# Retention outputs leave PSUM normalised by ScalarE instead of VectorE

## The reference, cut to what matters

```python
def retention(q, k, v, gn_g):
    ...
    scores = jnp.einsum('bnihd,bnjhd->bnhij', qc, kc) * decay
    inner = jnp.einsum('bnhij,bnjhe->bnihe', scores, vc)
    ...
    cross = jnp.einsum('bnihd,ih,bnhde->bnihe', qc, q_w, R_prev)
    o = (inner + cross).reshape(B, L, H, DV)
    mu = jnp.mean(o, axis=-1, keepdims=True)
    var = jnp.mean(jnp.square(o - mu), axis=-1, keepdims=True)
    o = ((o - mu) * lax.rsqrt(var + EPS)).reshape(B, L, H * DV)
    return o * gn_g.astype(jnp.float32)
...
    ret = retention(q, k, v, ret_gn_g[l]).astype(x.dtype) * jax.nn.silu(g_ret)
```

## Time and profile before

| | us |
|---|---|
| median of three runs | 2453.55 |
| the three runs | 2453.55, 2457.36, 2446.6 |
| the profiled execution, its own time | 2457.15 |
| its span, from the first to the last instruction | 2455.3 |
| busy in it: TensorE, VectorE, ScalarE, GpSimd | 2377.6, 1449.8, 679.2, 192.3 |
| mean granted TensorE clock | 0.992 of full speed |

### The profile page before, as it was taken

How to read it: one execution, slowest core, us unless ns; L and a number is a source line. 1 busy time by engine, 2 the same in 40 slices (tenths; PEclk the granted TensorE clock), 3 DMA queues, 4 the chain that set the end, 5 groups by cost and what they waited for, 6 DMA issues and landing times.

```text
span 2455.3 us, 35223 instructions
## 1 busy us (share of the span) xinstructions
PE 2377.6 (97%) x14746; PEld 1980.7 (81%) x14746; DVE 1449.8 (59%) x2462; ACT 679.2 (28%) x1096; POOL 192.3 (8%) x89
## 2 busy tenths in 40 slices
PE   7999999999999999999999998889999999999998
PEld 5887888887888788988877886777888888888887
DVE  5785259928896241471623542665566657777777
ACT  4211122124221021151423426341244432121123
POOL 1100000000000240202000000001000000000000
PEclk9999999999999999999999999999999999999999
DMA  7345652255577516332053342122145556434442
GB/s 232 124 143 178 211 173 102 90 188 177 172 243 222 178 56 214 137 108 103 22 206 100 122 164 84 55 76 104 51 169 187 181 200 215 139 136 137 133 146 90
DMA packets 269202, 354.30 MB, mean 144 GB/s; under 512 B 34962, under 2 KB 159859, under 8 KB 269043
## 3 DMA queue, kind: packets, MB, share of 16 engines
q1 hardware_dynamic: 236066, 301.56, 37.0%
q10 hardware_dynamic: 32976, 50.48, 5.6%
HBM read 244.93 MB, written 107.05 MB: 143 GB/s over the span
## 4 chain that ended last, share of the span: by engine, by line
PE 77%; DVE 10%; DMA 5%; ACT 3%; issue 3%; SPq 1%; ACTq 0%; DVEq 0%
PE PS L518 23%; PE PS L521 18%; PE PS L3381 14%; PE PS L3461 9%; DMA LAR<-ret_d 1%; PE PS L697 1%; DMA RAW<-in_w_gate_up 1%; PE PS L1966 1%; DVE W_LO L416 1%; PE PS L1982 1%; PE PS L2591 1%; DMA x_d<-X 1%; PE PS L1319 1%; PE PS L2586 1%; DMA CB<-pch_d 1%
## 5 line engine op out<-in xcount | busy, mean ns | idle before, releaser
L518 PE MATMUL PS<-W_HI,OP_HI 128*128 128x512 f32 (+1 forms) x1152 | 294.9, 399 | 3.2 <-DVE XO L1507 3.2
L518 PE MATMUL PS<-W_LO,OP_HI 128*128 128x512 f32 (+1 forms) x1152 | 280.1, 385 | 1.0 <-DVE W_LO L416 1.0
L518 PE MATMUL PS<-W_HI,OP_LO 128*128 128x512 f32 (+1 forms) x1152 | 278.9, 384 | 0.0
L451 POOL TENSOR_SCALAR W_HI<-RAW 128x2048 fp32r<-128x2048 f32 (+1 forms) x66 | 131.7, 2009 | 1528.6 <-PE PS L518 672.6
L518 PEld LDWEIGHTS PS<-W_LO,OP_HI 128*128 128x128 f32 x1152 | 213.9, 189 | 45.0 <-DVE W_LO L416 1.4
L518 PEld LDWEIGHTS PS<-W_HI,OP_HI 128*128 128x128 f32 x1152 | 209.9, 191 | 47.0 <-DVE OP_LO L1468 3.6
L518 PEld LDWEIGHTS PS<-W_HI,OP_LO 128*128 128x128 f32 x1152 | 212.6, 188 | 42.8 <-issue 0.5
L547 ACT ACTIVATE OST<-PS 128x512 f32<-128x512 f32 (+2 forms) x152 | 85.8, 564 | 440.8 <-PE PS L521 241.8
L416 DVE TENSOR_TENSOR W_LO<-RAW,W_HI 128x2048 fp32r<-128x2048 f32 (+1 forms) x58 | 138.5, 2405 | 81.1 <-POOL W_HI L451 61.7
L521 PE MATMUL PS<-OP_HI,W_HI 128*128 128x512 f32 x704 | 180.5, 398 | 0.0
L521 PE MATMUL PS<-OP_HI,W_LO 128*128 128x512 f32 x704 | 174.4, 390 | 0.0
(11 more groups left out here) (529 smaller groups left out, 3728.3 us busy)
## 6 DMA issues: line engine op xcount, KB each, us to landing
RAW<-in_w_gate_up SPq DMA_DIRECT2D x88, 512.0 KB, 5.9
RAW<-in_w_in SPq DMA_DIRECT2D x28, 1024.0 KB, 6.6
RAW<-in_w_out SPq DMA_DIRECT2D x12, 1024.0 KB, 8.5
LE<-spill_d SPq DMA_DIRECT2D x22, 512.0 KB, 4.5
RAWD<-in_w_down SPq DMA_DIRECT2D x11, 1024.0 KB, 4.9
X<-x_d SPq DMA_DIRECT2D x4, 2048.0 KB, 8.8
x_d<-X SPq DMA_DIRECT2D x2, 4096.0 KB, 18.2
ptok_d<-OST ACTq DMA_DIRECT2D x24, 256.0 KB, 2.0
```

The costliest lines, as they stand in the source:

```text
L451: nc.gpsimd.tensor_scalar(hi, raw, 1.0, 1.0, ALU.mult, ALU.mult).then_inc(*w_hi.by(1))
L518: ins = nc.tensor.matmul(PS[:, bank, 0:width], act_part[:, k, a * P:(a + 1) * P], w_part[:, slot, k, 0:width], start=start, stop=stop)
```

## The change: who writes the normalised outputs

The variance, its root and the reciprocal stay where they were. VectorE then forms, for all heads at once, minus the mean times the reciprocal root (`RNB`, 128 by 8), and signals `r_on`. ScalarE waits for that and writes `ONR`, head by head, with the function Identity, with the reciprocal root as the scale and `RNB` as the bias, each of them one number per partition; then it signals `r_on` again, which therefore counts to 2 per tile. The second signal is the one that TensorE waits for.

```diff
--- before.py
+++ after.py
@@ -68,7 +68,7 @@
 
 for later, earlier, total in (e.split() for e in (
         "gm r_turn 8, dec r_sc 8, tr r_o 8, la r_kv 7, c1 xw_lo 8, ex r_qkt 8, rt r_root 8, trc xv_hi 8, e1 r_trig 2,"
-        "ag r_scr 8, ss r_var 8, kk r_on 8, s r_rst 8, lt r_g 8, ct r_ang 1, in0 rq_in 128, in1 rv_in 128, v0 glu_z 16,"
+        "ag r_scr 8, ss r_var 8, kk r_on 16, s r_rst 8, lt r_g 8, ct r_ang 1, in0 rq_in 128, in1 rv_in 128, v0 glu_z 16,"
         "par rc_in 32,av s5_prm_t 1,q s5_cp_t 1").split(",")):
     SHARED["dn_" + later] = (earlier, int(total))
 
@@ -1605,6 +1605,7 @@
     BNS = at("BNS", "small", 2560, [P, RH, 6])
     BNM = at("BNM", "small", 2752, [P, RH, 2])
     RRS = at("RRS", "small", 2816, [P, 3, RH])
+    RNB = at("RNB", "small", 2912, [P, RH])
 
     rc_in, rq_in, rv_in, rg_in, rt_out = (sem(n) for n in ("rc_in", "rq_in", "rv_in", "rg_in", "rt_out"))
     r_ang, r_trig, r_ab, r_rot, r_turn, r_qkt, r_sc, r_scr, r_o, r_kv = (
@@ -1686,7 +1687,7 @@
             pe.wait_ge(*rv_in(16 * (t + 1)))
             pe.wait_ge(*r_rst(t + 1))
             if t:
-                pe.wait_ge(*r_on(t))
+                pe.wait_ge(*r_on(2 * t))
             place = lambda h: PS[:, 4 + h % 2, h // 2 * P:(h // 2 + 1) * P]
             for h in range(RH):
                 T.matmul(place(h), SCR[:, h % 2, h // 2, :], VL[:, h * P:(h + 1) * P], start=h < 2, stop=False)
@@ -1703,7 +1704,7 @@
             ins.then_inc(*r_kv.by(1))
 
         def turn_out(t):
-            pe.wait_ge(*r_on(t + 1))
+            pe.wait_ge(*r_on(2 * t + 2))
             if t + 1 < TT:
                 pe.wait_ge(*r_scr(t + 2))
             else:
@@ -1747,6 +1748,14 @@
             yield ret_time(t) + 0.6
             act.wait_ge(*r_var(t + 1))
             act.activation(RRS[:, 1, :], RRS[:, 0, :], ACT.Sqrt).then_inc(*r_root.by(1))
+            yield ret_time(t) + 0.8
+            act.wait_ge(*r_on(2 * t + 1))
+            if t:
+                act.wait_ge(*r_back(t))
+            for h in range(RH):
+                ins = act.activation(ONR[:, h, :], PS[:, 4 + h % 2, (h // 2) * P:(h // 2 + 1) * P], ACT.Identity,
+                                     bias=RNB[:, h:h + 1], scale=RRS[:, 2, h:h + 1])
+            ins.then_inc(*r_on.by(1))
             if t + 1 < TT:
                 yield ret_time(t) + 1.2
                 turned(t + 1)
@@ -1814,13 +1823,10 @@
 
         def normalize(t):
             dve.wait_ge(*r_root(t + 1))
+            if t:
+                dve.wait_ge(*r_on(2 * t))
             chain(V.reciprocal(RRS[:, 2, :], RRS[:, 1, :]))
-            if t:
-                dve.wait_ge(*r_back(t))
-            for h in range(RH):
-                ins = V.tensor_scalar(ONR[:, h, :], PS[:, 4 + h % 2, (h // 2) * P:(h // 2 + 1) * P],
-                                      BNM[:, h, 0:1], RRS[:, 2, h:h + 1], SUB, MUL)
-            ins.then_inc(*r_on.by(1))
+            V.scalar_tensor_tensor(RNB[:, :], BNM[:, :, 0], -1.0, RRS[:, 2, :], MUL, MUL).then_inc(*r_on.by(1))
 
         def gate(t):
             dve.wait_ge(*r_back(t + 1))
```

## The result

The changed kernel takes 2468.68 us (median of six runs, 2463.11 to 2473.7) where the kernel before, run beside it, takes 2454.32 (six runs, 2446.6 to 2457.36): 1.0058 times as long, with an interval of 1.0046 to 1.0071. In a later comparison it was 2471.14 against 2452.55, a ratio of 1.0080 [1.0065, 1.0095]. It is slower, by 14.4 and 18.6 us; forecast were 16.2. The profiled execution of the change took 2470.99, its span is 2469.2 and its mean clock 0.991.

A forecast was written before the change was run, and what follows sets the result against it. ScalarE's list order was taken to bound: the eight delay the sigmoid and `QKT`, so TensorE waits. Tile costs 4.6 + 2.6 + 2.0 + 4.8 + 0.3 + 1.9 = 16.2 on 2453.55 give about 2470 us, range 2457 to 2479.

The forecast's parts named there:

- ScalarE's list is what bounds: Main case, chance 0.66: ScalarE's list order is fixed and every tile lacks room, so slower, about 2470 us.
- the share of 28%: ScalarE's busy share, set aside as its room; 1.35 us in hand before tile 0's scores was taken instead.
- The price of the row: ScalarE's eight normalising instructions per tile: 455 ns each (278 + 89 + 88), 3.01 us a row; `RNB` on VectorE 0.20.
- the two cheaper rows: Lower prices for ScalarE's eight, 1.57 and 2.29 us a row, giving sums of 7.1 and 12.3 us.
- The waits: TensorE before the next scores, held by ScalarE's `QKT`: 3.03, 5.03, 2.0, 4.5, 0.3, 1.9 us at tiles 0-4 and 6.
- Mask waits go, VectorE idles before `GA`: TensorE's mask waits of 2.47 and 1.34 us vanish; VectorE's 2.4 us saved per tile goes into waiting for `GA`.
- The falls of the clock: TensorE's clock drops after longer waits, 1.6 us each, counted at tiles 0, 1 and 3.
- its upper end: Upper sum of 21.6 us: 16.2 plus 3.2 for falls at tiles 2 and 6 and 2.2 for tile 4.
- The end, with its 3.18, I take to move along: TensorE's 3.18 us wait before 818.46 stays, since loads and weight splits there wait on TensorE's units.
- the third case: Rival, chance 0.08: the end wait shrinks if loads do not move with TensorE, 16.2 - 3.2 - 1.7 = 11.3, so 2465 us.

The follow-up runs named there:

- a row of 1.47: The changed kernel with ScalarE's eight instructions copying without scale and bias, so outputs are not normalised: 2454.65 us, 1.0009 of the kernel before.
- the first profile: Profiled execution of the changed kernel (normalisation moved to ScalarE, against the kernel before): 2470.99 us; median of its six runs 2468.68.
- the second: The changed kernel run again unaltered, for a second profile: profiled execution 2474.18 us, median of six runs 2471.14, against 2452.55 before.

## Why the prediction was right, and where its steps were not

- **ScalarE's list is what bounds.** Right, and shown by place alone: 2442.5 with the eight behind, 2468.7 to 2471.1 with them in front. The view to read was the list, and not the share of 28%.
- **The price of the row.** 455 forecast, 465 measured; row 2.90 for 3.01; `RNB` 0.17 for 0.20. (By its own terms the two cheaper rows were 1.59 and 2.31, not 1.57 and 2.29, which changes nothing.) The rule of the Trainium skill (ScalarE: Activation LUTs, "What ACT_TABLE_LOAD costs") gave an estimate of 479 with two operands, and for none 293: the trace has 465 and 303. The rule of the Trainium skill that speaks for moving an eviction (VectorE: DVE Perf Modes, "Specifications") agrees only without operands, 303 against VectorE's 405, which has its two; with two, ScalarE's 465 is the dearer one. The time per instruction did not decide whether the kernel became slower: the same row stands in the slowest and in the fastest kernel here. Where the row stands in front of the others, it sets how much: 2454.65 with a row of 1.47.
- **The waits.** 3.0, 5.0, 2.0, 4.5, 0.3, 1.9 forecast; 1.82, 4.86, 1.77, 3.86, 1.35, 1.94 in the first profile and 2.93, 4.86, 1.78, 3.86, 0.54, 1.95 in the second. Tile 0's 1.82 is the first execution's own: TensorE came 1.3 late to it from the longer fall at 599.65. Of tile 3's 4.5, 0.6 were too many. Tile 4 was named as the uncertain one, with bounds of 0 and 2.5.
- **Mask waits go, VectorE idles before `GA`.** Right: behind the first mask none in either profile, and 19.7 us of idle time, in before 4.1 by the same view. The experiment with the copy in front showed what the prediction hadn't: once `QKT` no longer hid them, `GA` alone cost mask waits of 5.12 and 7.31, 3.3 of the latter beside GpSimd.
- **The falls of the clock.** Forecast behind tiles 0, 1 and 3. The first profile has them behind 1 and 3, the second behind five waits. Behind waits of about 1.8 to 2.0 it came or didn't; the prediction kept that for its upper end.
- **"The end, with its 3.18, I take to move along": this step failed.** The end gave 6.0 back in both profiles of the change, which is the third case, with a chance of 0.08. Its price of 3.2 + 1.7 was right for the wait and 1.1 too low for the fall. Both profiled executions came out near the 2470 all the same (2470.99 and 2474.18), since something stood against it each time: in the second extra falls at tiles 2 and 6 and a growth of 20.4 instead of 16.2, besides 2.3 ahead of the stretch and 2.8 behind it, which were not followed; in the first the 6.0 of entry and first fall. So the number was hit partly by luck, by errors of opposite sign; the direction was not.

**How the end went.** In the kernel before, VectorE's timeline has

```profile
813.29 4.42 DVE L1468 TENSOR_TENSOR OP_LO<-LAR,OP_HI 128x1024 fp32r<-128x1024 f32 x1 [7.58 <-ACT OP_HI L1462]
817.64 0.68 DVE L1507 TENSOR_TENSOR XO<-XI,PS 128x512 f32<-128x512 f32 x1
```

and GpSimd's, in the same kernel,

```profile
812.05 4.58 POOL L457 TENSOR_TENSOR W_LO<-RAW,W_HI 128x2048 fp32r<-128x2048 f32 x1
```

The split that takes 1.23 alone ended 1.1 after GpSimd's product did, at 817.71, and `XO`, for which TensorE waited, stood behind it. GpSimd's timeline of the changed kernel:

```profile
831.95 5.59 POOL L457 TENSOR_TENSOR W_LO<-RAW,W_HI 128x2048 fp32r<-128x2048 f32 x1
```

Here VectorE's split began at 831.85, 0.10 ahead; it took 1.23, and GpSimd's product became 1.0 longer. Against the last `turn_out`, GpSimd began at the same time in both kernels (14.15 behind it) and VectorE's split 1.3 earlier. In all seven profiles with `ONR` on ScalarE the split was first, by 0.06 to 0.98, and took 1.23 to 1.90; in both of the kernel before GpSimd was, by 1.24 and 0.77. Why the split comes earlier is only read, not tested: the chain of loads, copies and splits runs 1.4 earlier from tile 3's copy on (809.93, before 791.43), and ahead of that VectorE's addition at 807.17 (before 787.97, that is 807.87 with the 19.9 between the two) no longer stands behind eight normalisations, and SyncE's issue of two weight loads ended 2.3 earlier; how much each gives wasn't told apart.

## What to carry to other kernels

On an engine with a fixed list, ask of a moved piece of work not how long it takes there but what stands behind it and who waits for that: the same eight instructions made this kernel 0.6 to 0.8% slower in front of a copy and a sigmoid, and 0.4% faster than before behind them, in both with the wait at the end gone. Follow every consumer of what is delayed, since the one that waits longest hides the next. And a stall at the far end of a stretch may hang on which of two engines starts first, so don't take it to move along unless its whole chain does.

## What the runs showed of the hardware that was not expected

- VectorE's operations on two tensors in SBUF stood still beside GpSimd. The split of 1.23 took 4.42 and 4.89 when it began 1.24 and 0.77 behind GpSimd's product, so that it ended about 1.1 after it each time; begun 0.10 ahead, it took its 1.23. The two products above took 2.38 and 2.26 for 0.69. The Trainium skill (SBUF — State Buffer, "Who interferes with whom") has it that such an instruction and a GpSimd one that reads SBUF exclude each other, and that the order of issue decides who blocks; the traces agree with both.
- A wait of nearly the same length was followed by the lower clock in one execution and not in another: after 1.77, 1.82 and 1.94 none in the first profile of the change, after 1.78 and 1.95 one in the second; in the kernel before one after 2.47, and none after 2.49 in the variant with the addition moved. A fall costs 1.6 to 2.9 us in these rows, so the waits can be forecast better than the time.
